# One core, a hybrid decoder layer on 2,080 tokens: three programs in turn become one, the attention's values product swaps its operands, and the first slabs and the samples' work are reordered

## What is computed

```
proj = x @ w_in                       # q, k, v, o of 4 mLSTM heads; q of 8 window heads, k and v of 2
A: C = a*C + kw.T @ v ; h = (sc*q@C + (q@k.T * D) @ v) / max(|den|, exp(-m))     # mLSTM
B: s = q@k.T/8 + bias ; p = exp(s - mx) / (sum(exp(s - mx)) + exp(sink - mx)) ; o = p @ v   # window 128
x = LayerNorm(alpha * x + concat(A, B) @ w_out)
x = LayerNorm(alpha * x + (silu(x @ w_gate) * (x @ w_up)) @ w_down)
```

## Time and profile before

| what | before |
|---|---|
| median of 3 executions | 2575.45 us (2573.36 to 2578.94) |
| the profiled execution | 2576.87 us, of which the span of the records is 2575.1 us |
| PE busy | 2493.3 us, 97% of the span |
| DVE, ACT, POOL busy | 927.6, 937.3, 1287.1 us |
| DMA | 335.5 MB, mean 130 GB/s |
| mean granted clock of PE | 0.984 of full speed |

### The profile page before, as it was taken

How to read it: one execution, slowest core, us unless ns; L and a number is a source line. 1 busy time by engine, 2 the same in 40 slices (tenths; PEclk the granted TensorE clock), 3 DMA queues, 4 the chain that set the end, 5 groups by cost and what they waited for, 6 DMA issues and landing times.

```text
span 2575.1 us, 33629 instructions
## 1 busy us (share of the span) xinstructions
PE 2493.3 (97%) x13771; PEld 2427.3 (94%) x13771; DVE 927.6 (36%) x1535; ACT 937.3 (36%) x1415; POOL 1287.1 (50%) x544
## 2 busy tenths in 40 slices
PE   8989999999999988999999999999999999999997
PEld 7979999999999877899999999999999999999996
DVE  4345454444546444111424213421335114251104
ACT  3324444444455423222334224332244223342222
POOL 4444544445444434455545565555554555555552
PEclk9999999999999988999999999999999999999998
DMA  5443534434365663434334343344333443334331
GB/s 185 152 118 97 143 99 136 105 99 142 97 183 177 200 216 116 128 119 143 124 106 135 119 155 113 105 136 146 125 114 99 144 145 122 108 120 132 124 117 68
DMA packets 142480, 335.50 MB, mean 130 GB/s; under 512 B 14734, under 2 KB 79846, under 8 KB 141670
## 3 DMA queue, kind: packets, MB, share of 16 engines
q1 hardware_dynamic: 142326, 333.34, 41.4%
HBM read 305.05 MB, written 29.26 MB: 130 GB/s over the span
## 4 chain that ended last, share of the span: by engine, by line
PE 57%; DVE 2%; ACT 0%; issue 0%; ACTq 0%; DVEq 0%
PE l_acc L1670 19%; PE l_acc L1668 19%; PE l_acc L1669 19%; DVE l_total L1128 1%; DVE hl L1704 0%; PE var L1144 0%; PE mean L1140 0%; ACT nxt L1651 0%; DVE nxt L1763 0%; DVE part L1718 0%; DVE var L1765 0%; DVE hbuf L1700 0%; DVE nxt L1713 0%; ACT x_squares L1646 0%; DVE hh L1702 0%; DVE l_total L1718 0%
## 5 line engine op out<-in xcount | busy, mean ns | idle before, releaser
L1605 POOL TENSOR_TENSOR l_wlo<-l_raw,l_whi 128x1024 fp32r<-128x1024 f32 (+1 forms) x297 | 823.7, 2773 | 693.6 <-ACT l_whi L1614 693.6
L1614 ACT ACTIVATE l_whi<-l_raw 128x1024 fp32r<-128x1024 f32 (+1 forms) x297 | 340.8, 1148 | 1031.2 <-PE l_acc L1670 992.8
L253 POOL TENSOR_TENSOR wlo<-raw,whi 128x1024 fp32r<-128x1024 f32 x150 | 364.7, 2432 | 543.0 <-ACT whi L247 542.8
L1668 PE MATMUL l_acc<-xh,l_whi 128*128 128x416 f32 x1760 | 620.0, 352 | 7.9 <-PEq L1190 7.9
L1670 PE MATMUL l_acc<-xh,l_wlo 128*128 128x416 f32 x1760 | 621.9, 353 | 0.0
L1669 PE MATMUL l_acc<-xl,l_whi 128*128 128x416 f32 x1760 | 615.1, 350 | 0.0
L266 PE MATMUL acc<-xh,whi 128*128 128x416 f32 x1072 | 385.4, 359 | 0.0
L268 PE MATMUL acc<-xh,wlo 128*128 128x416 f32 x1072 | 378.1, 353 | 0.0
L267 PE MATMUL acc<-xl,whi 128*128 128x416 f32 x1072 | 375.5, 350 | 0.0
L1668 PEld LDWEIGHTS l_acc<-xh,l_whi 128*128 128x128 f32 x1760 | 331.0, 188 | 11.3 <-issue 8.8
L1669 PEld LDWEIGHTS l_acc<-xl,l_whi 128*128 128x128 f32 x1760 | 331.2, 188 | 6.7 <-issue 1.3
(11 more groups left out here) (333 smaller groups left out, 2567.6 us busy)
## 6 DMA issues: line engine op xcount, KB each, us to landing
l_raw<-in_wB SPq DMA_DIRECT2D x220, 512.0 KB, 3.6
raw<-in_wA SPq DMA_DIRECT2D x110, 512.0 KB, 3.7
l_raw<-in_w SPq DMA_DIRECT2D x80, 704.0 KB, 4.0
raw<-in_wB SPq DMA_DIRECT2D x40, 512.0 KB, 4.1
xraw<-in_xT SPq DMA_DIRECT2D x32, 416.0 KB, 5.6
xraw<-mixT SPq DMA_DIRECT2D x20, 416.0 KB, 6.5
stage<-in_xT SPq DMA_DIRECT2D x40, 208.0 KB, 4.2
pre<-stage SPq DMA_DIRECT2D x40, 208.0 KB, 4.1
```

Source lines behind the costliest of these rows:

```text
L253: self.nc.gpsimd.tensor_tensor(self.wlo[:, n % 4], self.raw[:, n % 4], self.whi[:, n % 3].bitcast(F32), ALU.subtract).then_inc(self.lo_don ...
L1605: nc.gpsimd.tensor_tensor(wlo[:, n % 4, 0:k], raw[:, n % 4, 0:k], whi[:, n % 3, 0:k].bitcast(F32), ALU.subtract).then_inc(S["lo_done"], 1)
L1614: nc.scalar.activation(whi[:, n % 3, 0:k], raw[:, n % 4, 0:k], ACT.Copy).then_inc(S["hi_done"], 1)
L1668: pe.matmul(bank, whi[:, n % 3, c], hx[:, a], start=(a == 0), stop=False)
```

## The change

1. **One program.** `mixers`, `tail` and `layer` return their engines' lists, which run in turn in one block. Semaphore waits stand where the barriers stood. `CUT` is 133.
2. **Values.** In p @ v the values are stationary (128x64) and p moves, 256 columns an instruction; the two key/value heads go to output partitions 0 to 63 and 64 to 127. The result is already turned, so `ow` and the transposes L660 are gone, and ACT copies it to the mix. p is scaled before its transposes: `normalise` on DVE, one 128x512 product for each of 4 window-head rows of a chunk.
3. **Pieces.** All chunks have their pieces at offsets (0,2,3,5,6,6). Chunk 14 starts at 119.
4. **First slabs.** The load of weight slab 3 is issued ahead of the loads of the constants, and half of the second token group is split before the first slab. The gate work stands one slab earlier, the stores of the gate rows one slab later, and the token load of visit 5 moves from slab 22 to 30 (its splits from 26..33 to 34..41).
5. **Samples.** Their loads are issued at slab 130. Their mix goes from DVE straight into the raw token tile, so the last token load is issued at 135 in place of 139, and its split is spread over 139 and 140 (before: all four quarters at 141).
6. **Norms.** Group 0: sum and mean 134 and 135 (before 138 and 139), the sum of squares 138, variance 140, scale 141, gain 142 (before 140, 141, 141, 142). The updates of the samples' state stand at 139 to 142 (before 143 to 146). In the layer VARIANCE moves from half-slab 5 to 6, SCALE 7, GAIN 8, HIGH 10, LOW 11. After the last slab, squares are summed by DVE additions, ACT squares and copies the mean, and POOL subtracts it from 4 of 8 tiles.

```diff
-CUT = PROJ + 3 * KD
+CUT = PROJ + 3 * KD - 1
-LOAD_X_AT = (None, None, 3, 6, 9, 22, 44, 66, 88, 110, 118, 126, 141)
+LOAD_X_AT = (None, None, 3, 6, 9, 30, 44, 66, 88, 110, 118, 126, 135)
-BASES = (24, 31, 37, 44, 51, 58, 66, 73, 80, 88, 94, 100, 106, 113, 120, 126)
-PIECES = tuple(tuple(b + o for o in (FIVE if c in (1, 9, 10, 11, 14) else SEVEN)) for c, b in enumerate(BASES))
+BASES = (24, 31, 37, 44, 51, 58, 66, 73, 80, 88, 94, 100, 106, 113, 119, 126)
+PIECES = tuple(tuple(b + o for o in (0, 2, 3, 5, 6, 6)) for b in BASES)
+SAMPLE_AT = BASES[-1] + 4
-        GATES_AT = 15
+    GATES_AT = 14
...
-                wait(pe, "p_exp", c, r + 1)
+            wait(pe, "p_normed", c, r + 1)
...
-            def window_values(c, r):
-                s = c % 2
-                wait(pe, "pt_copied", c, r + 1)
-                for gr in range(2):
-                    for half in range(2):
-                        last = pe.matmul(fb[:, r * P + gr * 64:r * P + gr * 64 + 64], ptw[:, r % 2, 2 * gr + half],
-                                         vs[:, s if half else 1 - s, gr * 64:gr * 64 + 64],
-                                         start=(half == 0), stop=(half == 1))
+        def window_values(c, pair):
+
+            s = c % 2
+            wait(pe, "pt_copied", c, 2 * pair + 2)
+            for half in range(2):
+                for gr in range(2):
+                    last = pe.matmul(fb[64 * gr:64 * gr + 64, pair * 2 * W:pair * 2 * W + 2 * W], vs[:, s if half else 1 - s, gr * 64:gr * 64 + 64],
+                                     ptw[:, :, 2 * gr + half], start=(half == 0), stop=(half == 1))
...
+        def normalise(v, c, pair):
+
+            s, a = c % 2, slice(4 * pair, 4 * pair + 4)
+            wait(dve, "snk_exp", c, pair + 1)
+            wait(dve, "p_exp", c, 2 * pair + 2)
+            v(nc.vector.tensor_tensor(snk[:, a], snk[:, a], psums[:, s, a], ALU.add))
+            v(nc.vector.reciprocal(snk[:, a], snk[:, a]))
+            for r in (2 * pair, 2 * pair + 1):
+                nc.vector.tensor_tensor(pw[:, r % 2], pw[:, r % 2], snk[:, 2 * r:2 * r + 2].unsqueeze(2).broadcast_to([P, 2, SPAN]),
+                                        ALU.mult).then_inc(S["p_normed"], 1)
...
-                nc.vector.tensor_tensor(ow[:].rearrange("p r (g d) -> p (r) g d", g=2), fb[:].rearrange("p (a d) -> p a d", d=64),
-                                        snk[:].unsqueeze(2).broadcast_to([P, 8, 64]), ALU.mult).then_inc(S["ow_ready"], 1)
...
+    norm_at = {"sum": CUT + 1, "mean": CUT + 2, "centre": CUT + 3, "square": CUT + 4, "sum_sq": CUT + 5, "variance": CUT + 7, "scale": CUT + 8, "gain": CUT + 9}
```

More of the change, by code:

```diff
@@ L1061 @@
-LAST_DVE = NC * 13
+    m = Store(nc, x.ring_at, X_AT)
+    ring = m.sb("ring", [P, NPROJ, RING])
+    xs = m.sb("xs_b", [P, H, 2, C])
+    bias = m.sb("bias", [P, 8, SPAN])
+    state, nlast, mix, mix_out, kv_out, st_out = (outs[n] for n in ("state", "nlast", "mix", "mix_out", "kv_out", "st_out"))
+    causal = m.sb("causal", [P, C])
+    ones = m.sb("ones", [P, 1])
+    sinks = m.sb("sinks", [P, 8])
+    gml = m.sb("gml", [P, H])
+    vaug = m.sb("vaug", [P, H, P + 1])
+    vs = m.sb("vs", [P, 2, P])
@@ new lines, in mixers @@
+    b, b_s = tile("b")
+    run, runs = tile("run")
+    u, us = tile("u")
+    em, ems = tile("em")
+    own = t.sb("own", [R, C])
+    gx, gxs = t.sb("xs", [R, 2, C]), t.sb("xss", [H, 2, NS])
+    ones_r = t.sb("ones_r", [R, C])
+    m_last = t.sb("m_last", [H, DB])
+    m_end = t.sb("m_end", [1, H])
+    ends = t.sb("ends", [1, 2, H, NC])
+    after = t.sb("after", [1, H, NC])
+    before = t.sb("before", [1, H, NC])
+    inherited = t.sb("inherited", [R, 1])
+    early = Store(nc, x.ring_at + EARLY * RING * 4, x.ring_at + NPROJ * RING * 4)
@@ L1064, in prompt_outputs @@
+    return sync, gpsimd, tensor, scalar, vector
+LAST_DVE = NC * 15
 def prompt_outputs(m):
@@ L1175, in layer_inputs @@
         "raw_in": [m.sem(f"l_raw_in{s}") for s in range(4)],
-        "norm": {n: m.sem("n_" + n) for n in Norm.SIGNALS},
         "S": {n: m.sem("l_" + n) for n in
@@ L1179, in layer_inputs, with tail @@
     }
-def tail(nc, io, keep, s_inp, outs, stream, ahead):
+def tail(nc, io, keep, s_inp, outs, stream, chunks, taken, ahead, norm, ps):
     cols, ident, sbias = keep["cols"], keep["ident"], keep["sbias"]
@@ L1519, in layer @@
-def layer(nc, io, keep, stream, ahead):
+    LAST = PROJ + 4 * KD - 1
+    FIRST, SCORES, HEADS, TURNED, OUT, UPDATES = (CUT + i for i in (0, 1, 2, 3, 4, 6))
+    HIGH_AT, FFN_AT = LAST + 2, LAST + 2
+    m = taken["rest"]
+    inp, (xs, state, n0, kc, vc, causal, sinkcol, gml) = s_inp, (
+        taken[n] for n in ("xs", "state", "n0", "kc", "vc", "causal", "sinkcol", "gml"))
+    expo = m.sb("s_expo", [NS, H, NS])
+    decay = m.sb("s_decay", [NS, H, NS])
+    prob = m.sb("s_prob", [NS, H, NS])
```

2494 lines of the change are left out of this document (1250 added, 1244 removed).

## The result

| | before | after |
|---|---|---|
| median, 4 executions each | 2577.19 us (2573.36 to 2581.67) | 2485.86 us (2485.2 to 2486.15) |
| profiled execution, span | 2576.87, 2575.1 us | 2485.81, 2484.0 us |
| PE busy; idle in the span | 2493.3; 81.8 us | 2447.8; 36.2 us |
| mean granted clock | 0.984 | 0.992 |

The ratio is 0.9645, with a 95% interval of 0.9628 to 0.9662: 91 us less. The forecast was 2477 with a range of 2462 to 2500.

What follows compares the result with a forecast made beforehand. PE, busy 97% of the span, was taken as the bound through its work, waits and clock. Terms 29.6 + 4.6 + 2.2 + 12.4 + 40 + 5.3 + 5.0 = 99.1 us off 2576.87 gave 2477 (by the median), range 2462 to 2500.

Steps and rivals of the forecast that it cites:

- Values, 29.6 us: p @ v in each chunk: column halves run together, 2 x 1.07 us in place of 3.99, over 16 chunks.
- The two rivals in which the halves run singly: p @ v: halves singly, gain 8.5 for 29.6, 2498, chance 0.09; singly with weight loads between, 2511, chance 0.03.
- New DVE work at nothing: Four 128x512 products a chunk on DVE cost no time, standing two slabs (9 us) ahead of the transposes that wait.
- The upper price: A DVE product of scaled p that meets POOL's subtraction takes about 2.2 us, against 0.69 from below.
- the even pieces at 4.6: All chunks spread alike: the five close chunks' waits go, 3.0 us for ACT and 1.6 for the state.
- The slower rival: turn_window waits for normalise at 32 places; above 3.1 us each the sign turns; at 3.5, 2588; chance 0.02.
- First slabs, 2.2 + 12.4: Start: wait for DVE's ring copy goes, 2.2 us; first chunk: gap of 9.36 and 3.1 of low clock go, 12.4.
- Tail, 40: Last chunk's OUT to the layer's first half-slab: 12 of 52 us of gaps and low clock stay, 40 go.
- The low clock at OUT: Samples' OUT, low clock without a gap: 4.5 us stays; a rival had it go with the updates' wait, 2470, chance 0.05.
- state 4.6: loads four slabs (18 us) earlier: Tail: PE's 4.6 us wait for the samples' state goes, as 3.1 MB loaded four slabs earlier take 9.4 us.
- the rival with the starved weight: Samples' loads at slab 130 delay the weight of slab 134: gap and low clock, up to 12 us, 2488; chance 0.08.
- Layer and end, 5.3 + 5.0: Layer's four waits for the sum of squares go, 5.3 us; after the last slab, wait, centring and mean save 5.0.

Runs made afterwards that it cites:

- the run with one half: Changed kernel, values matmuls issued by head and both heads written to output partitions 0 to 63, so all use one column half of PE: 2508.8 us.
- with the loads spread: Changed kernel, samples' loads over four slabs (130 to 133), and in slab 132 DVE's mixing product of the last chunk ahead of its split: 2479.57 us.
- the first run: Changed kernel, samples' loads spread over three slabs (130, 131, 132), each part behind the weight load of its slab: 2480.14 us.
- two orders of issue tried here: The changed kernel issues a values run's matmuls by key block, 2485.86 us; the same kernel with them issued by key/value head, 2486.93 us.

## Why the prediction was right, and where it was not

The time is 2485.9 where I said 2477: in the range, 9 us longer. The terms in turn:

- **Values, 29.6 us.** Right in mechanism and size: 2 x 1.02 = 2.04 us in place of 3.99. The scores of successive chunks come 1.8 us earlier each. The two rivals in which the halves run singly are refuted, and the run with one half shows what the first would have cost: 23 us, at 1.7 a chunk in the scores' times. The second, with the loads between them, had 2.16 us a run; even on one half it is 1.87. The rule of the Trainium skill that was weighed there ("TensorE: Matmul & The Clock Gate", Part 3: a weight load overlaps matmuls in flight only where the row group differs) does not describe this case, 1.02 against 1.87 us with all rows used in both.
- **New DVE work at nothing.** Right for the changed kernel, to within what can be measured, with the products at 0.69 us. The upper price, near which the prediction had them, did not come: they start ahead of POOL's subtraction, not within it. But the reason given, two slabs of room, is a condition that another part of the change creates. I had costed the even pieces at 4.6 (the waits that they take away) and missed that without them the new chain would make new ones: 14.5 us on the kernel before. The two terms are not additive. That their sum came out right is luck in this: the change had both.
- **The slower rival** (turn_window waiting for the scaling) is a real mechanism: at nine of ten places in close chunks it costs up to 3.0 us on the kernel before, just at the 3.1 from which, at all 32 places, it would have decided the sign. In spread chunks it costs nothing.
- **First slabs, 2.2 + 12.4.** Right in mechanism and size. The order on SP is worth 12.4 by the starts around it, in the changed kernel and alone on the kernel before; between the medians of that run it is 9.0, and in its profiled execution 2.8 us were lost ahead of this work. Undone in the changed kernel it cost 10.5, since the gap that came back was 6.4 us long and not 9.4. The wait for `ring` is gone with the earlier fourth weight, though no run moved that load alone.
- **Tail, 40.** Over its own stretch the term is right: 149.9 us before and 109.5 now (the sign given was 110), with no wait above 1.4. Both borders, the sum of squares and the split are gone, and 2.7 is left at the updates (2.3 foreseen). The low clock at OUT stayed, at about half of its cost.
- **The step that failed** is in this term: "state 4.6: loads four slabs (18 us) earlier", at no price but the 9.4 us of their transfer. The wait for the state did go, but I asked only when the 3.1 MB would land, and put at nothing what their move costs ahead of the tail. It cost the last chunk 12.7 us, 35.0 for the 24.2 of before less 1.95 for its values, and with the loads spread it is down to 23.0. (The sum had 111.6 for the tail, 38 of the 40 off, so that the two together are 10 short.) That was the rival with the starved weight, which I gave 0.08 at 2488; the time came out at 2485.9. Two things were mis-sized there. The first is SP's own time: the issue of four state transfers took it 5.83 us, and the weight was issued at 826.49, 5.5 us after the end of the slab that frees its buffer (130, at 821.0 by PE's pitch; the 819 that I had written ahead of the first run was an error of mine). The second is the slack: I counted four slabs to PE's use of the weight, but ACT's copies for the current slab stand behind its rounding in ACT's list, so the slack that counted was two slabs shorter.
- **What no run separates:** what one program is worth by itself, since none put a barrier back, and whether the wait at the border to the layer went with the barrier or with the earlier norm.
- **Layer and end, 5.3 + 5.0.** Right for the layer: 5.2 us of waits and 6.0 us of time with the number undone. At the end it is 5.4 us, in the traces alone, as no run undid that part, where the reciprocal now starts 6.1 us behind the last slab matmul's start (11.5 before).

```profile
2473.11 2.75 DVE L1807 RECIPROCAL w<-root 128x416 f32<-128x416 f32 x1
```

The range held because the one large miss was among the rivals whose times it took in.

## What to carry to other kernels

When loads are moved earlier, price what stands behind them in the issuing queue and in the list of the engine that consumes the next transfer: the first victim here was a copy that needed no transfer at all. A longer chain ahead of a matmul is free only with slabs between its pieces, so the spacing and the chain are one term and are to be costed together. And a small matmul that fills half of the columns is worth pairing with one on the other half; of the two orders of issue tried here neither was better.

## What the runs showed that was not expected

- Two chains of fp32 matmuls on different column halves overlap even where one chain is issued behind the other: 1.02 us a run in both orders, 1.87 on one half.
- The issue of a weight's transfer on SP took 0.33 us in many slabs, but 1.58 behind the state's four in the changed kernel and 2.61 in the first spread version; the four took 5.83. The next weight's, 3.7 us later in the changed kernel, took 0.44 with the DMA still at 0.98 of its share, so what sets it is open. An SP list has a rate of its own.
- A short wait of PE costs more than itself at the full clock too: ten waits of 8.5 us in all cost 12.7.
- A DVE product that starts ahead of a POOL subtraction is not slowed by it, 1.01 us for a split; one that starts within it took 2.5.
- In the changed kernel the clock fell behind gaps as short as 1.3 us (low pitch from 909.5 to 912.2 and from 925.4 to 929.1). Behind the 1.9 us wait for em_s it fell in seven of the ten profiled executions made from the changed kernel (139.9 to 143.3 with the layer's variance back) and not in the changed kernel's own. At the samples' OUT it fell without a gap, before and after alike. Why it falls there was not tried.
